# Scatter behind the gate/up products and the next expert's bias ahead of the down products, in a top-4-of-32 expert layer

## What is computed

```python
logits = (h @ router_w) + router_b
top_val, top_idx = lax.top_k(logits, TOP_K)          # 4 of 32 experts per token
top_w = jax.nn.softmax(top_val, axis=-1)
...
gu = xb @ w_gu[e] + b_gu[e]                          # 1024 -> 2048
g = jnp.minimum(gu[:, :D_FF], SWIGLU_LIMIT)
u = jnp.clip(gu[:, D_FF:], -SWIGLU_LIMIT, SWIGLU_LIMIT)
a = (u + 1.0) * (g * jax.nn.sigmoid(SWIGLU_ALPHA * g))
return a @ w_dn[e] + b_dn[e]                         # 1024 -> 1024
...
y = zeros.at[slot_tok].add(ys * slot_w[:, None])     # back to the tokens, weighted
```

## Time and profile before

| | us |
|---|---|
| device time, median of 3 runs (lowest to highest) | 1334.62 (1334.13 to 1336.18) |
| the profiled execution, its span | 1336.8 |
| TensorE busy within the span | 1240.6 |
| expert part, from the first bias product to the end of the last down products | 339.6 to 1325.4 |
| bytes read from HBM | 454.58 MB |

### The profile page before, as it was taken

One profiled execution on the slowest core, in us unless ns is written; L12 is line 12 of the kernel. 1 busy time (PEld: TensorE's weight loads), 2 busy tenths in 40 slices (PEclk: granted clock), 3 DMA queues, 4 the chain that ended last, 5 costly groups with the idle time before them and its releaser, 6 DMA issues.

```text
span 1336.8 us, 16801 instructions
## 1 busy us (share of the span) xinstructions
PE 1240.6 (93%) x6611; PEld 635.5 (48%) x6611; DVE 274.5 (21%) x495; ACT 274.3 (21%) x555; POOL 220.7 (17%) x95
## 2 busy tenths in 40 slices
PE   7999997998999999999999999999999999999996
PEld 6999886887433333333333333333333333333332
DVE  3155363323211111111111111111111111111112
ACT  5545364343200110010011001100100110001002
POOL 6776664774000000000000000000000000000000
PEclk9999998989899999999999999999999999999998
DMA  9655543766799999999999999999999999999960
GB/s 323 201 168 163 189 128 96 269 219 232 302 385 417 410 416 417 410 398 418 405 417 410 417 390 414 404 420 406 419 404 417 412 394 417 408 409 415 408 269 32
DMA packets 117027, 456.23 MB, mean 341 GB/s; under 512 B 7317, under 2 KB 47949, under 8 KB 84188
## 3 DMA queue, kind: packets, MB, share of 16 engines
q1 hardware_dynamic: 116812, 455.42, 86.6%
q0 software_dynamic: 176, 0.26, 0.1%
HBM read 454.58 MB, written 1.07 MB: 341 GB/s over the span
## 4 chain that ended last, share of the span: by engine, by line
PE 82%; DVE 11%; issue 2%; ACT 2%; POOL 2%; DMA 1%; SPq 0%; DVEq 0%; ACTq 0%; POOLq 0%
PE ps L477 78%; DVE arena L1211 2%; DVE arena L1206 2%; DVE arena L1209 2%; DVE arena L1202 2%; PE ps L733 2%; POOL w_parts L464 2%; DVE arena L1203 1%; DMA arena<-in_w_mem_kv 1%; PE ps L728 1%; ACT arena L856 1%; DVE arena L1087 1%; PE ps L522 1%; DVE row_max L1097 1%; DVE neg_max L1104 0%
## 5 line engine op out<-in xcount | busy, mean ns | idle before, releaser
L477 PE MATMUL ps<-arena,gathered_T 128*64 128x512 f32 x2048 | 456.1, 598 | 0.0
L477 PE MATMUL ps<-arena 128*64 128x512 f32 (+5 forms) x1482 | 354.1, 615 | 31.2 <-DVE arena L1211 30.3
L477 PEld LDWEIGHTS ps<-arena,gathered_T 128*64 128x64 f32 x2048 | 142.2, 137 | 289.0 <-issue 288.2
L477 PEld LDWEIGHTS ps<-arena 128*64 128x64 f32 (+3 forms) x1482 | 129.5, 158 | 227.0 <-issue 219.1
L464 POOL TENSOR_TENSOR w_parts<-arena,w_parts 128x1024 fp32r<-128x1024 f32 x84 | 211.4, 2542 | 96.2 <-ACT w_parts L836 95.4
L1202 DVE TENSOR_SCALAR arena<-ps 128x512 f32<-128x512 f32 x32 | 22.1, 692 | 814.8 <-PE ps L477 814.8
L836 ACT CAST w_parts<-arena 128x1024 fp32r<-128x1024 f32 x82 | 81.9, 1048 | 122.0 <-PE ps L477 119.5
L477 PE MATMUL ps<-w_parts,h_T_parts 128*128 128x256 f32 x816 | 102.0, 283 | 0.2 <-POOL w_parts L464 0.2
L477 PEld LDWEIGHTS ps<-w_parts,h_T_parts 128*128 128x128 f32 x816 | 99.1, 188 | 4.3 <-issue 3.0
L954 ACT COPY arena<-ps 128x512 f32<-128x512 f32 x32 | 18.8, 586 | 298.9 <-PE ps L477 298.9
L949 ACT COPY arena<-ps 128x256 f32<-128x256 f32 x32 | 11.9, 373 | 330.0 <-PE ps L728 330.0
(11 more groups left out here) (156 smaller groups left out, 578.5 us busy)
## 6 DMA issues: line engine op xcount, KB each, us to landing
arena<-in_expert_w_gate_up SPq DMA_DIRECT2D x256, 1024.0 KB, 8.2
arena<-in_expert_w_down SPq DMA_DIRECT2D x128, 1024.0 KB, 9.5
arena<-in_w_in SPq DMA_DIRECT2D x29, 1024.0 KB, 5.4
arena<-in_w_mem_kv SPq DMA_DIRECT2D x4, 1024.0 KB, 13.7
arena<-in_w_out SPq DMA_DIRECT2D x4, 1024.0 KB, 9.6
arena<-t_scratch SPq DMA_DIRECT2D x6, 384.0 KB, 4.0
arena<-in_w_branch_a SPq DMA_DIRECT2D x2, 1024.0 KB, 5.1
arena<-in_w_branch_c SPq DMA_DIRECT2D x2, 1024.0 KB, 5.0
```

The costliest lines, as they stand in the source:

```text
L477: return nc.tensor.matmul(out, lhsT, rhs, start=start, stop=stop, **kw)
```

## The change

The bias products leave `expert` and become `bias_rows`. `expert` takes a function `next_bias`, which issues the bias of expert n+1 between the activation transposes and the wait for `aT_ready`. The bias of expert 0 is issued once ahead of the loop. The scatter of expert n-1 leaves its place after chunk 3 and now comes after chunk 7, ahead of `gather`; `open_sums` moves with it. The wait for `y_ready` stays after chunk 3. Since the last expert has no next bias, the last four experts are written out behind the loop, whose passes go from 7 to 6. The overflow part keeps its own order. Programs of the other engines are unchanged.

```diff
--- before.py
+++ after.py
@@ -692,14 +692,7 @@
 
             WT_of = [None]
 
-            def expert(n, c, fills, wt_slot, bias_slot, bias_fill, xt, xt_fill, gather, wait_rows=None):
-
-                def slot(j):
-                    return ring_slot(c + j)
-
-                def chunk_landed(j):
-
-                    pe.wait_ge(landed[slot(j)], (fills + ((c + j) // RING + 1 + front_fills(slot(j)))) * 16)
+            def bias_rows(n, bias_slot, bias_fill):
 
                 pe.wait_ge(brow_in[bias_slot], bias_fill)
                 pe.wait_ge(gu_drained, n + 1)
@@ -707,6 +700,16 @@
                     for h in range(2):
                         mm(ps[64 * h:64 * h + 64, b, :], ones[64 * bias_slot:64 * bias_slot + 1, 0:BLK],
                            brow[64 * bias_slot:64 * bias_slot + 1, b * D + 512 * h:b * D + 512 * (h + 1)], True, False)
+
+            def expert(n, c, fills, wt_slot, xt, xt_fill, gather, next_bias, wait_rows=None, one_wt=False):
+
+                def slot(j):
+                    return ring_slot(c + j)
+
+                def chunk_landed(j):
+
+                    pe.wait_ge(landed[slot(j)], (fills + ((c + j) // RING + 1 + front_fills(slot(j)))) * 16)
+
                 if wait_rows:
                     wait_rows()
                 for k in range(KC):
@@ -717,21 +720,26 @@
                                       ring[:, slot(k), b * D + 512 * h:b * D + 512 * (h + 1)], False, k == KC - 1)
                     last.then_inc(chunk_used, 1)
                     if k == 3:
-                        if WT_of[0] is None:
-                            open_sums()
-                        else:
+                        if WT_of[0] is not None:
                             pe.wait_ge(y_ready, n)
+                        if one_wt:
                             scatter()
-                        WT_of[0] = WT[:, wt_slot, :]
                         pe.wait_ge(PW_ready, n + 1)
                         for tt in range(T):
                             last = nc.tensor.transpose(ps[:, 3, tt * P:(tt + 1) * P], PW[:, tt, :], ident[:])
                         last.then_inc(WT_ps, 1)
+                if WT_of[0] is None:
+                    open_sums()
+                elif not one_wt:
+                    scatter()
+                WT_of[0] = WT[:, wt_slot, :]
                 gather()
                 pe.wait_ge(act_ready, n + 1)
                 for f in range(4):
                     last = nc.tensor.transpose(ps[:, 2, f * P:(f + 1) * P], sig[:, f * P:(f + 1) * P], ident[:])
                 last.then_inc(aT_ps, 1)
+                if next_bias:
+                    next_bias()
                 pe.wait_ge(aT_ready, n + 1)
                 pe.wait_ge(XT_ready, xt_fill)
                 for j in range(KC, EXPERT_CHUNKS):
@@ -761,7 +769,7 @@
             pe.wait_ge(normed, 3)
             gather_half(0, 2 * BLK)
             gather_half(1, 2 * BLK, 2)
-            def four_experts(it):
+            def four_experts(it, last_four=False):
                 for q in range(4):
                     n = it * 4 + q
 
@@ -773,12 +781,17 @@
                     def wait_rows():
                         pe.wait_ge(XT_ready, n + 2)
 
-                    expert(n, EXPERT_CHUNKS * q, it * 3, q % 2, q % 2, (it * 2 + (q // 2 + 1)) * 16,
+                    def next_bias():
+                        bias_rows(n + 1, (q + 1) % 2, (it * 2 + ((q + 1) // 2 + 1)) * 16)
+
+                    expert(n, EXPERT_CHUNKS * q, it * 3, q % 2,
                            XT[:, q // 2, :, BLK * (q % 2):BLK * (q % 2) + BLK], n + 3, gather,
-                           None if q % 2 else wait_rows)
+                           None if last_four and q == 3 else next_bias, None if q % 2 else wait_rows)
+            bias_rows(0, 0, 16)
             four_experts(0)
-            with pe.Fori(1, EXPERTS // 4) as it:
+            with pe.Fori(1, EXPERTS // 4 - 1) as it:
                 four_experts(it)
+            four_experts(EXPERTS // 4 - 1, True)
             n_over = pe.value_load(ovf[0:1, MAX_OVERFLOW:MAX_OVERFLOW + 1], min_val=0, max_val=MAX_OVERFLOW)
             with pe.If(0 < n_over):
                 with pe.Fori(0, MAX_OVERFLOW) as b:
@@ -792,8 +805,9 @@
                             gather_half(half, BLK)
                         pe.wait_ge(XT_ready, b * 2 + (EXPERTS + 4))
                         WT_of[0] = WT[:, 1, :]
-                        expert(n, 0, b + EXPERTS * EXPERT_CHUNKS // RING, 1, 0, (b + (EXPERTS // 2 + 1)) * 16, XT[:, 0, :, 0:BLK], b * 2 + (EXPERTS + 4),
-                               lambda: pe.wait_ge(WT_ready, n + 1))
+                        bias_rows(n, 0, (b + (EXPERTS // 2 + 1)) * 16)
+                        expert(n, 0, b + EXPERTS * EXPERT_CHUNKS // RING, 1, XT[:, 0, :, 0:BLK], b * 2 + (EXPERTS + 4),
+                               lambda: pe.wait_ge(WT_ready, n + 1), None, one_wt=True)
             pe.wait_ge(y_ready, EXPERTS)
             with pe.If(0 < n_over):
                 pe.wait_ge(y_ready, n_over + EXPERTS)
```

## The result

| | device time, us | against before (95% interval) |
|---|---|---|
| before | 1334.38 (1332.51 to 1336.18, 4 runs) | |
| changed | 1305.05 (1302.12 to 1305.55, 4 runs) | 0.9773 (0.9761 to 0.9786) |

The kernel is 2.2% faster, 29 us. The forecast was 1292 (1283 to 1308): the right way and the right mechanism, with 13 us too much hope. 1305 lies outside the 1285 to 1299 that carried a chance of 0.68; the wider range holds it because it was drawn to take in rival 1. The profiled execution of the changed kernel took 1304.99 us, its span is 1303.2.

What follows compares the result with a forecast made beforehand. TensorE bounds before, the DMA after: first landing 372.7 plus 903.3 us of loads gives 1276.0, TensorE's end 1281.6, plus 11.4 is span 1293.0; less 2.2 is 1290.8, with 1.7 for a clock fall 1292 us (1283 to 1308).

Steps and rivals of the forecast that it cites:

- rival 1: DMA has nothing in reserve: stream stays 918.5 us, sign 410 GB/s, time 1305.5; chance 0.17 together with rates between.
- What bounds now, and the two idle pieces: TensorE sets the pace; its waits for VectorE before activation transposes (0.86 us) and down products (0.97 us) go: 27.8 us an expert.
- The falls of the clock: TensorE dropping from 2.4 to 1.2 GHz after idle stretches, 0.92 us an expert on average; taken to be gone.
- the written-out last four experts: Code behind the loop: cost of fetching it taken as 0, bounds -1 and +5 us.
- What is late next: DMA becomes the bound; its 28 us lead shrinks 2.4 us an expert, then TensorE waits at `brow_in` after 8 to 10 experts.
- Expert and bias are 12.591 MB: at 417 GB/s 30.2 us: DMA's pace per expert from its window rate; 376.7 MB from expert 2's first landing then take 903.3 us.
- The end: After the last chunk lands at 1276.0, TensorE finishes at 1281.6 and 11.4 us follow, giving span 1293.0.
- From span to device time: Profile span lies 2.2 us above the runs' median, so predicted device time was 1334.6 - 43.8 = 1290.8 us.
- my own sign: Mark of the forecast being right in the DMA's rate: 415 to 418 GB/s.
- Rival 2: The DMA isn't the bound: TensorE keeps 27.8 us periods to the end, time about 1246; chance 0.05.
- Rival 3: Long DMA queue lowers its rate: slower than before below 397 GB/s, 1353 us at 390; chance 0.04 shared with another rival.
- Rival 4: TensorE's clock keeps falling: 1294 us, or 1350 if twice an expert; slower outcome's chance 0.04, shared with another rival.

Runs made afterwards that it cites:

- e8: Kernel before the change, loading only the first half of each down chunk: 1334.7 us.
- e7: Changed kernel, with the bias row of expert n+1 loaded behind chunk 3 of expert n: 1299.4 us.
- e5: Changed kernel, with each bias row loaded as 16 separate pieces of 512 B, 132 floats apart in SBUF: 1297.85 us.
- e6: Changed kernel, with each bias row loaded three times into three rows of SBUF: 1332.4 us.
- e2: Kernel before with only the scatter's move; the bias stays at the head of its own expert: 1299.7 us.
- e4: Changed kernel, loading only the first half of each down chunk: 1234.5 us.
- e3: Kernel before with only the bias's move; the scatter stays after chunk 3: 1309.5 us.
- e9: Changed kernel with the bias row spread in 16 pieces and loaded ahead, and down chunks in 8 KB packets: 1285.7 us.
- e10: Kernel before with only the scatter's move, plus the bias row spread in 16 pieces and down chunks in 8 KB packets: 1284.2 us.

## Why the prediction was right, and where its 13 us are

*What bounds now, and the two idle pieces.* Right. e8 shows TensorE as the bound of before; both waits of the earlier trace rows are gone, and an expert takes 27.47 us where I had 27.8. The third of a microsecond lies in closer hand-overs: the bias starts 0.53 us after the transposes (I had 0.60), the transposes 1.89 after the gather (1.98), the gate/up products 6.91 after the down products (7.01). The falls of the clock went with the idle pieces, as I took it, and came back only with the pause at the bias. Nothing was lost at the written-out last four experts: TensorE's only idle pieces there are the waits for the bias row and, in the last expert, the 0.84 us for VectorE.

*What is late next.* Right in kind: TensorE first stops in its ninth expert (I had 8 to 10), at `brow_in`. The number was luck: 28 us of lead at the 2.4 us an expert that I had make 11.7, and what made it nine are the measured 30.5 - 27.5 = 3.0. That this does not starve the DMA is right too (e7, the same stream).

*The step that was mis-sized: "Expert and bias are 12.591 MB: at 417 GB/s 30.2 us".* Measured 30.48. The window rate is a mean over 16 engines; a chunk has landed when the last engine is done. The 8 KB bias row is one piece on one engine, e5 gives 30.27 without that, e6 31.31 with three of them. The stream took 911.9 us instead of 903.3: 8.6 us. In the middle of it the rate is 417 as I had it, because the other engines run ahead; the last engine is 10.3 us behind the first at the end, and over the whole stream the same bytes make 413. In e5 both are smaller together: 3.9 us of drift, and 2.3 us over 903.3. So the row in one piece is 6.3 of the 8.6 us; the other 2.3 have no experiment. I had counted the bias as 8 KB of bytes and not as a packet in one engine's line. The Trainium skill has the rule on the page "DMA: Bandwidth & Descriptors" (Why a DMA increments its semaphore by 16, on how many engines a DMA uses): the number of engines is the largest up to 16 that divides the slowest dimension above 1 that the instruction carries, and a contiguous row can be split by software so that it is spread. The runs agree: the changed kernel's instruction carries one element of 8192 B, that of e5 16 of 512 B, and 6.3 us of stream lie between them. That rule should have been put to the 8 KB row beforehand.

*The end.* From the last landing I had 17.0 us, it was 19.0. The down products of expert 30 took 8.78 us instead of 7.09, a fall of the clock behind the pause, as in the row of 890.81 above (I had put 1.2 us for it outside of the span). e7 and e2, without the pause, have 15.7 and 15.6.

*From span to device time: 4 us.* I subtracted 2.2 us, because the span of before lay that much above the median. In the runs since, each profiled execution is known with its own time, 1.8 to 2.0 us above its span (1304.99 and 1303.2 here). If that held before too, the execution profiled there was about 4 us slower than the median, and my sum should have added 1.8. Together: 8.6 + 2.0 + 4.0, less 0.4 for the first landing and the 1.2 that I had added, is 13.0.

*The rivals.* The number of rival 1 (1305.5) came true by coincidence, its reason only in part. "The DMA has nothing in reserve" would be a stream of 918.5 us; there were 911.9, and 905.6 with the row spread, 897.5 with larger packets too. What I had named as its sign, 410 GB/s, was not there, and my own sign, 415 to 418 GB/s, was, although my number was off. Rival 2 is refuted by the wait for the bias row and by e4: freed of the DMA the kernel takes 1234.5 us, which the changed kernel misses by 70 (I had 1246, with 27.8 us an expert instead of 27.47). Rival 3 did not occur for the long queue as such: 417 GB/s with 22 us from issue to landing. It needs one engine with more to do, as in e6. Rival 4: the clock did fall again, but only where there was a pause too. In e4 and e7 the one-row bias stands at the same place without one, and the clock stays at 1.00 (400 to 1180 us in e4). With an idle piece ahead of it, as in e3, it fell in 23 of 30 experts, more often than before the change.

## What to carry to other kernels

When TensorE and the loads are both near full, taking idle pieces out of TensorE's order pays only up to the loads' pace; work that pace out before, and expect a part of the edit to bring the whole gain if it alone takes TensorE below that pace soon enough. e2 did, e3 did not, because the clock kept falling. Take the pace from landings, not from the mean rate: one small load in a full queue, if it is one contiguous row, costs the whole stream time: here 0.2 us in every 30.5. And where an engine must wait for the loads anyway, let it wait late and often rather than early and once: a wait ahead of work whose data is already there shows up at the end, and here as a fall of TensorE's clock.

## What the runs showed of the hardware that was not expected

- The landings of one chunk on the 16 engines drift apart when the queue never empties: 0.4 us at expert 2, 10.3 us at the end with the bias row on one engine, 3.9 us with it spread. A mean rate doesn't see it: 417 GB/s from 555 to 860 us in both.
- In e6 the drift stopped at 11 to 12 us, and from there the whole DMA slowed to about 400 GB/s. Why an extra row cost 0.42 us an expert there ((31.31 - 30.48) / 2) and only 0.21 in e5 (30.48 - 30.27) is not settled; that the other engines run dry in e6 is the likely part of it, but was not tried apart.
- Two rows of 4 KB in one packet of 8 KB took a down chunk from 2.55 us to 2.49.
- From 376 to 460 us an issue of SyncE takes 0.33 us for a gate/up chunk and 0.38 for a down chunk (medians). From 600 to 1200 us, with the longer queue, it is 0.88 and 4.1 (the row of 1257.6 above), and in e9 and e10, with down chunks in rows of 8 KB, 1.9 for either. What holds the issue up was not tried, and no run shows a cost of it.
- An idle piece of 0.9 us is followed by a fall of the clock at one place (e3, 23 of 30 experts) and one of 0.8 to 1.0 us at another is not (e2, none from 400 to 1280 us).
